# Tile 0's experts in four parts, front steps moved to the v rows, the prompt norm's scale and shift on ACT: a streaming encoder with PEER layers on one core

## The reference

```python
def peer_ffn(h, w_pq, sub_keys, u_tab, v_tab):
    q = (hf @ w_pq).reshape(n, PEER_HEADS, 2, PEER_HALF)            # 8 heads, two halves of 128
    s = jnp.einsum('nhjd,hjkd->nhjk', q, sub_keys)                  # 128 keys in each half
    sv, si = lax.top_k(s, PEER_TOPK)                                # 16 of 128
    cand = (sv[:, :, 0, :, None] + sv[:, :, 1, None, :]).reshape(n, PEER_HEADS, 256)
    cidx = (si[:, :, 0, :, None] * PEER_NKEYS + si[:, :, 1, None, :]).reshape(n, PEER_HEADS, 256)
    tv, ti = lax.top_k(cand, PEER_TOPK)                             # 16 of 256
    eidx = jnp.take_along_axis(cidx, ti, axis=-1).reshape(n, 128)
    gate = jax.nn.softmax(tv, axis=-1).reshape(n, 128)
    a = jnp.einsum('tkd,td->tk', u_tab[ei], hx)
    w = gt * jax.nn.gelu(a, approximate=False)
    return jnp.einsum('tk,tkd->td', w, v_tab[ei])

# in run_trunk, for each of 2 layers
    sh1, sc1, gt1, sh2, sc2, gt2 = ada_mod(c, w_ada[l], b_ada[l])
    h = rmsnorm(x, g_norm[l, 0]) * (1 + sc1) + sh1
    z = h @ w_in[l]                                                 # pooling, gMLP and attention inputs
    ...
    y = jnp.concatenate([ya, yb, o.reshape(B, T, ATT_WIDTH)], axis=-1) @ w_out[l]
    x = x + gt1 * y
    h2 = rmsnorm(x, g_norm[l, 1]) * (1 + sc2) + sh2
    x = x + gt2 * peer_ffn(h2, w_pq[l], sub_keys[l], u_tab[l], v_tab[l])
```

## Time and profile before

| | us |
|---|---|
| median of three runs | 2733.89 |
| lowest, highest | 2730.05, 2742.97 |
| the profiled execution, its own time | 2736.93 |
| its span | 2735.0 |
| PE, DVE, POOL busy in it | 1353.5, 1517.9, 1469.3 |
| u rows' dots (L664), 768 | 906.3 |
| v rows' batches (L1076), 192 of 16 matmuls | 582.5 |
| DMA moved | 969 MB, 354 GB/s |

### The profile page before, as it was taken

How to read it: one execution, slowest core, us unless ns; L and a number is a source line. 1 busy time by engine, 2 the same in 40 slices (tenths; PEclk the granted TensorE clock), 3 DMA queues, 4 the chain that set the end, 5 groups by cost and what they waited for, 6 DMA issues and landing times.

```text
span 2735.0 us, 22105 instructions
## 1 busy us (share of the span) xinstructions
PE 1353.5 (49%) x7726; PEld 752.6 (28%) x7726; DVE 1517.9 (55%) x3242; ACT 205.5 (8%) x529; POOL 1469.3 (54%) x1542
## 2 busy tenths in 40 slices
PE   4977383686423253455565375688420023333544
PEld 2756272553113221223211065464100000000111
DVE  1326789957558965455350489856857764443000
ACT  1221012010000001000000011111000000000000
POOL 0000435446665555666666654446666666666664
PEclk8989685798656566777776587698655555556676
DMA  7987688899999989999999999799999999999997
GB/s 283 368 306 312 253 329 322 319 364 388 357 383 359 408 341 368 370 401 410 399 372 365 366 373 346 267 367 351 326 380 386 371 360 371 366 368 365 363 371 300
DMA packets 265893, 969.15 MB, mean 354 GB/s; under 512 B 38036, under 2 KB 40084, under 8 KB 262456
## 3 DMA queue, kind: packets, MB, share of 16 engines
q0 software_dynamic: 221184, 805.40, 77.4%
q1 hardware_dynamic: 42256, 161.25, 15.5%
q10 hardware_dynamic: 2344, 1.09, 0.2%
HBM read 962.36 MB, written 5.27 MB: 354 GB/s over the span
## 4 chain that ended last, share of the span: by engine, by line
DVE 23%; POOL 20%; PE 19%; issue 16%; another core or an unknown queue 12%; DMA 7%; ACT 1%; ACTq 1%; SPq 0%; DVEq 0%; POOLq 0%
DVE ring L664 12%; POOL ring L379 12%; POOL ring L374 8%; PE ps L1281 5%; PE ps L1076 3%; DMA ring<-in_v,eV 3%; PE ps L1118 3%; DMA ring<-in_u,eU 2%; PE ps L1256 1%; PE ps L980 1%; DMA wada<-in_wada 1%; PE ps L1122 1%; DVE ti L918 1%; ACTq L399 1%
## 5 line engine op out<-in xcount | busy, mean ns | idle before, releaser
L664 DVE CUSTOM_DVE_ANT_0 ring<-ring,ps 128x1024 f32<-128x1024 f32 x768 | 906.3, 1218 | 510.5 <-DMA ring<-in_u,eU 342.0
L374 POOL DMA_INDIRECT ring<-in_u,eU x768 | 728.2, 948 | 795.2 <-DVE mods L621 234.1
L379 POOL DMA_INDIRECT ring<-in_v,eV x768 | 736.9, 959 | 396.4 <-issue 212.9
L1076 PE MATMUL ps<-ring,Wd 128*32 128x512 f32 x3072 | 582.5, 893 | 695.8 <-DMA ring<-in_v,eV 632.7
L1076 PEld LDWEIGHTS ps<-ring,Wd 128*32 128x32 f32 x3072 | 118.5, 140 | 1091.9 <-issue 1087.9
L1118 PE MATMUL ps<-h,wring 128*128 128x128 f32 (+1 forms) x768 | 149.8, 359 | 139.7 <-issue 66.3
L1281 PE MATMUL ps<-h,wring 128*128 128x128 f32 (+1 forms) x1024 | 197.0, 348 | 25.9 <-DMA wring<-in_wpq 12.9
L1281 PEld LDWEIGHTS ps<-h,wring 128*128 128x128 f32 x1024 | 166.7, 204 | 79.9 <-issue 52.2
L1118 PEld LDWEIGHTS ps<-h,wring 128*128 128x128 f32 x768 | 131.3, 215 | 156.6 <-issue 113.1
L868 DVE MAX8 sv<-sc 128x8 f32<-128x128 f32 x192 | 50.0, 288 | 182.8 <-ACT sc L386 101.2
L682 DVE SCALAR_TENSOR_TENSOR x<-ps,mods,x 128x128 f32<-128x128 f32 x32 | 8.6, 343 | 217.6 <-PE ps L1084 186.9
(11 more groups left out here) (167 smaller groups left out, 1128.0 us busy)
## 6 DMA issues: line engine op xcount, KB each, us to landing
wada<-in_wada SPq DMA_DIRECT2D x24, 2048.0 KB, 12.7
wring<-in_win SPq DMA_DIRECT2D x72, 512.0 KB
wring<-in_wpq SPq DMA_DIRECT2D x64, 576.0 KB
wring<-in_wout SPq DMA_DIRECT2D x32, 512.0 KB
ring<-in_u,eU POOLq DMA_INDIRECT x768
ring<-in_v,eV POOLq DMA_INDIRECT x768
wring<-in_ckT SPq DMA_DIRECT2D x8, 512.0 KB
wring<-in_cv SPq DMA_DIRECT2D x8, 512.0 KB
```

What stands on the lines that cost most here:

```text
L374: g.indirect_dma_start(ring[p % NR][:], None, a["u"], bass.IndirectOffsetOnAxis(ap=eU[t % 3][:, i:i + 1], axis=0)).then_inc(ld_r[p % NR], 16)
L379: g.indirect_dma_start(ring[p % NR][:], None, a["v"], bass.IndirectOffsetOnAxis(ap=eV[t % 3][:, tok:tok + 1], axis=0)).then_inc(ld_r[p % N ...
L664: nc.vector.tensor_tensor_reduce(ring[p % NR][:], ring[p % NR][:], ps[:, 0:2, :].rearrange("p b d -> p (b d)"), 1.0, 0.0, ALU.mult, ALU.ad ...
L1076: ins = mm(ps[QUAD * q:QUAD * q + QUAD, 2 + half, :], Wd[:, QUAD * q + c, :], ring[at4[q] % NR][:, half * 512:(half + 1) * 512], start=(c ...
```

## The change

**Tile 0's experts in parts.** PARTS_OF = (4, 1, 1, 1, 1, 1): `experts` gets a part. For tile 0 DVE does heads 0 and 1 behind pq step 4, heads 2 and 3 behind step 8, and so on, each part followed by 16 dots (`gathers(16 * part)`), and part 3 comes behind step 15's top-k. POOL waits for `eu_done` every 32 rows of tile 0. Softmax on ACT comes in four parts. `tokens(0)` moves to pq step 3 on PE.

**Buffers of the start.** So that rows can come before the modulation is complete, `wada` 0 lies in `Wd`'s space, `wada` 1 and 2 in ring buffers 11 to 14 and 7 to 10; `brev` and the bias's small tensors lie in ring buffers 0 to 5. Loads 20 to 23 all use `wada` 0. POOL's wait for mods_done 12 goes; at position 7 it waits for product 19. `Wd` is zeroed by ACT (`clear`) behind unit 0 instead of by POOL at the start. ADA_AT is new; the flips and the bias's copies move from before the first norm to ticks 10 to 15.

**Room.** A position with a u row counts 1, one with a v row 2, in `tick_at`; unit 1's stretch starts at 64 instead of 0.

**The prompt norm.** DVE multiplies x with 1/rms; scale and shift are eight Identity activations on ACT (L483 of the new kernel).

```diff
+PARTS_OF = (4,) + (1,) * (TILES - 1)
+EP0 = tuple(sum(PARTS_OF[:t]) for t in range(TILES + 1))
...
-SPAN = ((0, 0), (0, AT["u", T0[1] * P]), (RES_OF[0] + 1, AT["v", 2 * P] + HEAD - 16), (RES_OF[2] + 1, AT["u", T0[3] * P]))
+EARLY = 16
+SPAN = ((0, 0), (4 * EARLY, AT["u", T0[1] * P]), (RES_OF[0] + 1, AT["v", 2 * P] + HEAD - 16), (RES_OF[2] + 1, AT["u", T0[3] * P]))
 def tick_at(n, k):
     a, b = SPAN[n]
     cost = COST[:T_EXP + 8 * NT[n]]
-    return a + (b - a) * sum(cost[:k + 1]) // sum(cost)
+    room = [1 if kind == "u" else 2 for kind, _ in ORDER[a:b]]
+    share, p = sum(room) * sum(cost[:k + 1]), 0
+    while p < b - a and sum(room[:p + 1]) * sum(cost) <= share:
+        p += 1
+    return a + p
-ADA_AT = {2: (4,), 6: (5,), 10: (6,), 14: (7,), 19: (8,), 20: (9, 10), 22: (11, 12), 24: (13, 14), 27: (15,), 29: (16,), 34: (17,), 36: (18,), 40: (19,),
-          44: (20,), 48: (21,), 50: (22,), 51: (23,)}
+ADA_AT = {2: (4,), 5: (5,), 8: (6,), 19: (7, 8), 20: (9, 10), 22: (11, 12), 24: (13, 14), 27: (15,), 29: (16,), 31: (17,), 35: (18,), 37: (19,),
+          40: (20,), 43: (21,), 46: (22,), 49: (23,)}
+ADA_SLOT = [x % ADA_BUF if x < 20 else 0 for x in range(ADA_N)]
+FLIP_AT = {10: 0, 11: 1, 12: 2, 13: 3, 14: 4, 15: 5}
...
-        wada = [at(f"wada{s}", [KD, 512], G0 + s * 16384) for s in range(ADA_BUF)]
-        brev = [at(f"brev{k}", [H, keys[k]], WD + (0, 4096, 6144)[k]) for k in range(3)]
+        wada = [at(f"wada{s}", [KD, 512], (WD, G0 + 11 * 4096, G0 + 7 * 4096)[s]) for s in range(ADA_BUF)]
+        brev = [at(f"brev{k}", [H, keys[k]], G0 + (0, 4096, 6144)[k]) for k in range(3)]
...
             g.wait_ge(flip_pe, 6)
-            g.memset(Wd[:], 0.0).then_inc(wd_zero, 1)
-            g.wait_ge(mods_done, DEPTH * NMOD)
...
+                if p == 7:
+                    g.wait_ge(adm_pe, 20)
                 if kind == "u":
-                    if i == 0:
-                        g.wait_ge(eu_done, t + 1)
+                    if i * PARTS_OF[t] % P == 0:
+                        g.wait_ge(eu_done, EP0[t] + i * PARTS_OF[t] // P + 1)
...
+            def clear():
+                act.wait_ge(hist_zero, 1)
+                act.wait_ge(adm_pe, ADA_N)
+                copy(Wd[:].rearrange("p q m -> p (q m)"), zaE[1][:, 0, 0:1].broadcast_to([P, P * QUAD])).then_inc(wd_zero, 1)
...
                 act.activation(r, r, ACT.Sqrt).then_inc(rt_done, 1)
+                if g:
+                    m = mods[l]
+                    for k in range(KD):
+                        act.wait_ge(xn_done, 4 * l + 2 * w + k // 4 + 1)
+                        ins = act.activation(hg[1][:, k, :], hg[1][:, k, :], ACT.Identity, bias=m[:, 3 * w * KD + k, 0:1], scale=m[:, (3 * w + 1) * KD + k, 0:1])
...
+                    if n == 0 and u and u % 4 == 0:
+                        experts(n, 0, 0, u // 4 - 1)
+                        gathers(EARLY * (u // 4))
                 topk(2 * PH - 1)
                 for i, t in enumerate(tiles):
-                    experts(n, i, t)
+                    for k in range(8 if n == 0 else 1):
+                        tick(n, T_EXP + 8 * i + k)
+                    experts(n, i, t, PARTS_OF[t] - 1)
+                if n == 0:
+                    gathers(4 * EARLY)
...
-            def experts(n, i, t):
+            def experts(n, i, t, part):
+                size = PH // PARTS_OF[t]
+                hs = slice(part * size, (part + 1) * size)
...
-                step(nc.vector.tensor_copy(eU[t % 3][:], eF[:]), eu_done)
-                dve.wait_ge(texp_done, t + 1)
+                step(nc.vector.tensor_copy(eU[t % 3][:, ks], eF[:, ks]), eu_done)
+                dve.wait_ge(texp_done, EP0[t] + part + 1)
...
-                if n == 0:
-                    pe.wait_ge(bias_done, 1)
-                else:
+                if n:
                     pe.wait_ge(sc_ev, 2 * PH * n)
...
+                    if n == 0 and u == 3:
+                        tokens(0)
```

More of the change, by code:

```diff
@@ L160, in build @@
         eF = own("eF", [P])
-        ysb = own("ysb", [D])
+        cT = own("cT", [KD, 32])
+        YS = room(D * 4)
+        ysb = at("ysb", [D], YS)
         wring = [own(f"wring{s}", [WSLOT]) for s in range(NWR)]
@@ L569, in front, with softmax @@
                 root(n, 1)
+                def softmax(t, part):
+                    act.wait_ge(tvs_done, EP0[t] + part + 1)
+                    v = tv[:, part * PH // PARTS_OF[t]:(part + 1) * PH // PARTS_OF[t], :]
+                    act.activation(v, v, ACT.Exp).then_inc(texp_done, 1)
                 def scores_out(u):
@@ L586, in front @@
                         scores_out(u - 1)
+                    if n == 0 and u % 4 == 2 and u > 4:
+                        softmax(0, u // 4 - 1)
                 scores_out(2 * PH - 1)
@@ L629, in _, with bias_part @@
             modulation(1)
[L630 removed]
+            def bias_part(f):
                 k, half = f // 2, f % 2
                 dve.wait_ge(flip_pe, f + 1)
[L633 to L636 removed]
+                step(nc.vector.tensor_copy(bias[k][:, 2 * half:2 * half + 2, :].rearrange("p h k -> p (h k)"), ps[:, 7, 0:2 * keys[k]]), flip_ev)
+                if f == 5:
+                    nc.vector.memset(bias[1][0:CHUNK, :, CHUNK:P], NEG)
+                    step(nc.vector.memset(bias[2][0:CHUNK, :, P + CHUNK:2 * P], NEG), bias_done)
             at_ = [0]
@@ L708, in norm @@
                     m = mods[l]
+                    r = rs[:, 0:N]
+                    if g:
+                        dve.wait_ge(ss_pe, 2 * n + w + 1)
+                        step(ts(r, ps[:, 6, 0:N], 1.0 / D, EPS, ALU.mult, ALU.add), ms_done)
+                        dve.wait_ge(rt_done, 2 * n + w + 1)
+                        step(recip(r, r), chain)
+                        for k in (0, 4):
+                            tt(h[:, k:k + 4, :], x[:, k:k + 4, :], r.unsqueeze(1).broadcast_to([P, 4, N]), ALU.mult).then_inc(xn_done, 1)
+                        return
                     for k in (0, 4):
@@ L920, in experts @@
                     if half == 0:
-                        tick(n, T_EXP + 8 * i + 3)
-                        for h in range(PH):
+                        between(3)
+                        for h in heads:
                             ins = nc.vector.match_replace(flat[h], tv[:, h, k], flat[h], -3e38)
                         step(ins, chain)
-                tick(n, T_EXP + 8 * i + 6)
-                step(nc.vector.tensor_copy(st[:, 144:152], tv[:, :, 0]), chain)
-                step(tt(tv[:], tv[:], st[:, 144:152].unsqueeze(2).broadcast_to([P, PH, TOPK]), ALU.subtract), tvs_done)
@@ L929, in experts @@
[L929 to L935 removed]
+                between(6)
@@ new lines, in experts @@
+                top = st[:, 144 + part * size:144 + (part + 1) * size]
+                step(nc.vector.tensor_copy(top, tv[:, hs, 0]), chain)
+                step(tt(tv[:, hs], tv[:, hs], top.unsqueeze(2).broadcast_to([P, size, TOPK]), ALU.subtract), tvs_done)
+                step(ts(ta[:, hs], ti[:, hs], 4, None, ALU.logical_shift_right), chain)
+                step(ts(tb[:, hs], ti[:, hs], 15, None, ALU.bitwise_and), chain)
+                step(nc.vector.tensor_copy(taf[:, hs], ta[:, hs]), chain)
@@ L952, in _ @@
+                step(red(top, tv[:, hs], AX.X, ALU.add), chain)
+                step(recip(top, top), chain)
+                ins = tt(gate[t % 3][:, ks].rearrange("p (h k) -> p h k", h=size), tv[:, hs], top.unsqueeze(2).broadcast_to([P, size, TOPK]), ALU.mult)
+                step(ins, sel_done if part + 1 == PARTS_OF[t] else chain)
             front(0)
-            modulation(DEPTH * NMOD - 1)
             front(1)
```

131 lines of the change are left out of this document (72 added, 59 removed).

## The result

The change makes the kernel slower: 2775.94 us against 2735.23 us (medians of four runs each), a ratio of 1.0145, 95% interval 1.0122 to 1.0169. Forecast were 2717 us and a range up to 2756. The profiled execution of the changed kernel has a span of 2769.6 us, 34.6 more than before.

A forecast was written before the change was run, and what follows sets the result against it. The kernel was taken as a DMA stream of rows with holes where front chains hold it up; −12 (unit 1), −6 (unit 2), +1 (unit 3) took 2736.9 to 2720, or 2717 at the median; stated range 2684 to 2756.

The forecast's parts named there:

- First row 71 us sooner: Unit 0, tile 0 in parts: part 0's eU at 225, first dot at 229 instead of 300.
- Unit 0's end at 363: Unit 0 on DVE: 16 dots end near 254, three rounds of 36 us follow, ending near 363 with 64 dots done.
- Last dot at 469: Unit 1's u rows: six dots, norm, 58 dots and z take DVE 106 us, so the last dot comes at 469.
- The sign that I had named for being wrong: Between the 64th dot by 363 and the 128th near 469: DVE idle over 15 us would show the forecast wrong.
- The v stretch of 254 us: Unit 1 behind the last dot: gelu, attention, out, norm2, pq and experts, with no dots to hide behind, sum to 254 us.
- X1: End of unit 1's chain, tokens(1): forecast at 723 us, against 722.25 before.
- 12 us for the full ring: Behind unit 1: 15 rows stand ready, so row 247 comes at 729 instead of 740.7; 12 us won, plus or minus 10.
- Unit 2, 6 us: Unit 2: some five pq chunks and their loads move into its last 104 v rows; 6 us won, bounds 0 and 12.
- Unit 3, one us lost: Unit 3: u stretch 167 us instead of 184, v stretch 218, tokens(4) near 1977; one us lost, plus or minus 8.
- (c): Rival, chance 0.17: v stretches of units 1 and 3 outlast the rows, batches take 3.63 us at half clock; 2760 us.
- ACT's norm at a few us either way: Unit 1's norm: DVE saves 4.9 us; ACT's eight operations take 3 us, 1.5 on the path, at most 3.
- The rule on turns between queue rows: First burst of rows: DMA engines alternate between queue rows, so no long waits; nothing charged, though 16 us would cancel the gain.

The follow-up runs named there:

- e11: Changed kernel with EARLY = 0: four parts, no early dots, unit 1's stretch from position 0, v rows still counting 2; ratio 1.0143 to the kernel before.
- e7: Changed kernel with four parts kept, no early dots, u and v rows counted alike, unit 1's stretch from position 0; ratio 0.9950 to the kernel before.
- e5: Changed kernel with tile 0's experts in one part, unit 1's stretch from position 0, u and v rows counted alike; ratio 0.9988 to the kernel before.
- e6: Changed kernel with the prompt norm's scale and shift on DVE again; ratio 1.0161 to the kernel before.
- e4: Changed kernel with tile 0's experts in one part, no early dots, unit 1's stretch from position 0, weights kept; ratio 1.0174 to the kernel before.

## Why the prediction was wrong

The forecast was 17 us faster on the profile's own time and the profile came out 34.6 slower. Of these 51 us, 32 fall to unit 1 and 25 to unit 3; the tail wins 5 back.

*First row 71 us sooner:* nearly right. Part 0's eU came at 228.71, forecast 225; the first dot at 239.72, forecast 229, since the first row took 10 us, not 4.5.

*Unit 0's end at 363:* wrong by 19. Part 0's 16 dots ended at 262, not 254, and the three rounds behind them took 120 us, not 109. (By the forecast's own rates, 1.24 to 1.42 us a row, the dots would have ended by 252.) Of the 11 us in the rounds 6 lie in the first one: the top-k of steps 4 to 7 took 13.3 us (262.36 to 275.58) where I had 7.4. In it DVE stood 6.0 us, in steps 5 and 6, whose scores ACT had copied by 225.1; ACT's own stand, to 272.78, bears on step 7 alone. What DVE stood for is not in the trace. The dots were no cover for PE either: what kept PE's next chunks was not the score bank that I had named but the modulation, behind the dots on DVE (262.10).

*Last dot at 469:* this is the step that failed. The weights stand at 500.92, so the last dot came near 500: 19 us late from unit 0 and 13 more from unit 1's u stretch. The sum took DVE as full for 106 us behind unit 0, and it was busy 104.67 of 119, with one stand of 12.47 us in z; from 229 to 382 128.6 of 153. A stretch in which DVE is the busiest engine is not one in which it is full: before, too, it was 66.0 of 73 and 105.8 of 118, and I read these as full. The sign that I had named for being wrong, over 15 us of idle DVE on the way to the 128th dot, came: 24 and 14 us in the two windows.

*The v stretch of 254 us:* right in its length. It took 249: 89 for attention, out and norm2 (forecast with gelu 100), 85 for pq (83), 75 for the experts (71 with stalls). The v stretch before had taken 156 us (565.71 to 722.25), so 93 were lost here. The forecast needed the last dot 97 us sooner to make up for that, and it came 65 sooner. I compared only the two ends, 723 and 722, and did not weigh whether the u stretch could win back so much.

*12 us for the full ring:* the mechanism was right. The dots behind tokens(1) waited for DMA first at 764.08, on the same row 249, 14.0 us behind it, before 21.8: 8 us. But tokens(1) was 28 us later, so this row came 20 us later, not 12 sooner.

*Unit 2, 6 us:* the lag goes from 19 us at position 288 to 12 at 768, 7 us won. In e11, with the same weights, it is 6, in e7 without them 1 us more of a lead. About right, though the late stream of the first two makes it no clean comparison.

*Unit 3, one us lost:* wrong by 25, in part by the same step. The u stretch took 188 us, not 171 (167 and 4 for gelu): DVE was busy 162.64 of it, near the 167, and stood 14.56 at the norm's mean alone. My base was misread besides: before, the stretch from the residual to the weights took 205 us and not the 184 that I lessened to 167, which is why "near 1750 instead of 1779" is 29 us sooner and not 17. So 17 us were won, as many as the forecast took off, but from a longer stretch. The v stretch took 232 us, not 218, before 181: in all 31 more than forecast. That tokens(4) would be met by a full ring was right, and did not help.

*The rivals.* (c) had the sign, the place and the point from which it decides (X1 above 735), and at 2760 it was nearest; but its price rested on half-clock batches, and these are not the cause. From 501 to 590, where attention and the output product lie, the granted clock was 0.90 and eight of nine batches took 1.92 us; from 590 to 675 it was 0.98 and a batch took the 1.92 us of the earlier trace rows:

```profile
609.08 1.92 PE L1150 MATMUL ps<-ring,Wd 128*32 128x512 f32 x16
```

The length comes from steps that wait for one another, which I had written down in the forecast itself (254 us) and not held against the 181 and 156 us of before.

*ACT's norm at a few us either way, the flips, the buffers:* right, e5 and e6 show nothing of them in the time.

*The rule on turns between queue rows.* ACT's stand came again, to 272.78, 5.6 us behind the burst's last issue at 267.20, but of its 44 us all but 4.7 are PE's, whose product was done at 268.04. So what a burst could have cost here is some 5 or 6 us, not 16, and I had charged nothing. The Trainium skill, "DMA: Bandwidth & Descriptors", section "Queues, rings and completion order", by whose turns between queue rows, as I read them, no other transfer would wait long, would have left such a charge out; what ACT and DVE waited for is not in the trace, so the rule is neither borne out nor refuted.

## What to carry to other kernels

Work that runs on another engine beside a chain fills the chain's gaps; moving the chain away from it doesn't shorten the chain, it only lays the gaps bare. Before steps are moved from one stretch to another, add up both stretches, before and after, with each one's floor (here about 146 us of rows against a chain of 215), and take the larger for each. A lead at the start is worth only what the slowest chain behind it can use: 62 us of it changed nothing where the next unit's front was the limit (e4), and 0.4% with even weights and no early dots (e5 to e7), which the intervals do not quite part.

## What the runs showed of the hardware

The first row's fetch took 10 us from issue to use when a 2 MB load, and weight loads behind it, had been issued 2 us ahead of it, against 4.5 on a DMA that had little else to do (0.08 busy from 260 to 296):

```profile
227.94 0.33 SPq L310 DMA_DIRECT2D wada<-in_wada  x1
```

And in three kernels ACT stood in the first burst of gathers although PE's product for it was done: before, 16.6 us, to 342.33; changed, 4.7 us, to 272.78; in e7, where the burst was 15 rows long, 11.8 us, to 255.79. Each stand ended 1 to 6 us behind the burst's last issue (336.81, 267.20, 254.72). In the changed kernel DVE stood too, 6.0 us between 265 and 273. What they waited for no run showed.
